# One 512-wide matmul for the high and low token parts of the two convolved up projections, with half of each low weight part made by an adding DMA

## The reference

```python
def conv_ffn(h, w_in, conv_w, conv_b, w_out):
    z = causal_dwconv(h @ w_in, conv_w, conv_b)   # 3 taps per channel, along the tokens
    u, g = jnp.split(z, 2, axis=-1)               # 2816 channels each
    return (jax.nn.gelu(g) * u) @ w_out
```

## Time and profile before

| | |
|---|---|
| median of 3 runs | 1712.98 us |
| the profiled execution | 1715.28 us, of which the span from first to last instruction is 1713.5 us |
| granted TensorE clock, mean | 0.998 |
| PE busy | 1697.4 us (99%) |
| DVE busy | 1380.2 us (81%) |
| ACT busy | 998.8 us (58%) |
| POOL busy | 28.3 us (2%) |
| DMA | 367.06 MB, 214 GB/s over the span |

### The profile page before, as it was taken

How to read it: one execution, slowest core, us unless ns; L and a number is a source line. 1 busy time by engine, 2 the same in 40 slices (tenths; PEclk the granted TensorE clock), 3 DMA queues, 4 the chain that set the end, 5 groups by cost and what they waited for, 6 DMA issues and landing times.

```text
span 1713.5 us, 29104 instructions
## 1 busy us (share of the span) xinstructions
PE 1697.4 (99%) x11410; PEld 1538.4 (90%) x11410; DVE 1380.2 (81%) x2142; ACT 998.8 (58%) x1596; POOL 28.3 (2%) x39
## 2 busy tenths in 40 slices
PE   8999999999999999999999999999999999999999
PEld 8799998999998988889998798888888888698888
DVE  5778888888888888899986879888988876866654
ACT  6565545776554555446678756553655356865542
POOL 0200000000000000000000200000000000000000
PEclk9999999999999999999999999999999999999999
DMA  9345558544547777794552157779687844045552
GB/s 347 136 163 196 180 221 311 190 157 171 196 173 274 277 285 280 281 367 177 173 193 100 50 172 287 277 273 358 241 289 278 312 170 177 27 149 195 195 181 90
DMA packets 62436, 367.06 MB, mean 214 GB/s; under 512 B 6944, under 2 KB 7328, under 8 KB 27776
## 3 DMA queue, kind: packets, MB, share of 16 engines
q1 hardware_dynamic: 61776, 362.70, 58.0%
q0 software_dynamic: 560, 3.01, 0.4%
HBM read 364.64 MB, written 1.05 MB: 213 GB/s over the span
## 4 chain that ended last, share of the span: by engine, by line
PE 92%; DVE 4%; ACT 3%; issue 1%; DMA 0%; SPq 0%; POOLq 0%; DVEq 0%; ACTq 0%; POOL 0%
PE psum L517 18%; PE psum L538 13%; PE psum L390 11%; PE psum L392 11%; PE psum L391 11%; PE psum L519 9%; PE psum L540 6%; PE psum L445 4%; PE psum L507 2%; DVE lo L1934 1%; PE psum L585 1%; ACT hi L1276 1%; PE psum L510 1%; PE psum L986 1%; PE psum L912 1%
## 5 line engine op out<-in xcount | busy, mean ns | idle before, releaser
L1934 DVE TENSOR_TENSOR lo<-raw,hi 128x1024 fp32r<-128x1024 f32 x522 | 621.4, 1229 | 163.0 <-ACT hi L1276 162.9
L1276 ACT ACTIVATE hi<-raw 128x1024 fp32r<-128x1024 f32 x522 | 523.2, 1052 | 334.8 <-PE psum L540 191.5
L517 PE MATMUL psum<-XHL,hi 128*128 128x512 f32 x1280 | 452.5, 399 | 0.0
L390 PE MATMUL psum<-XHL,hi 128*128 128x256 f32 x1320 | 375.9, 285 | 0.1
L391 PE MATMUL psum<-XHL,hi 128*128 128x256 f32 x1320 | 373.5, 283 | 0.0
L392 PE MATMUL psum<-XHL,lo 128*128 128x256 f32 x1320 | 373.5, 283 | 0.0
L519 PE MATMUL psum<-XHL,lo 128*128 128x256 f32 x1280 | 359.5, 281 | 0.0
L538 PE MATMUL psum<-HHL,hi 128*128 (+1 forms) x960 | 338.8, 398 | 0.4 <-DVE S L2124 0.4
L517 PEld LDWEIGHTS psum<-XHL,hi 128*128 128x128 f32 x1280 | 240.5, 188 | 59.9
L540 PE MATMUL psum<-HHL,lo 128*128 (+1 forms) x960 | 269.1, 280 | 0.0
L390 PEld LDWEIGHTS psum<-XHL,hi 128*128 128x128 f32 x1320 | 253.2, 192 | 2.5 <-issue 1.6
(11 more groups left out here) (342 smaller groups left out, 2029.0 us busy)
## 6 DMA issues: line engine op xcount, KB each, us to landing
raw<-slabs_dram SPq DMA_DIRECT2D x269, 1024.0 KB, 5.2
modw<-wmod_dram SPq DMA_DIRECT2D x144, 512.0 KB, 5.4
raw<-slabs_dram SPq DMA_DIRECT2D x4, 512.0 KB, 7.7
A<-small_dram POOLq DMA_DIRECT2D x1, 1536.0 KB, 12.5
X<-x_dram SPq DMA_DIRECT2D x4, 256.0 KB, 4.9
out_dram<-X SPq DMA_DIRECT2D x3, 256.0 KB, 2.3
cond<-cvec_dram POOLq DMA_DIRECT2D x1, 512.0 KB, 7.6
A<-tab_dram POOLq DMA_DIRECT2D x1, 512.0 KB, 15.7
```

The costliest lines, as they stand in the source:

```text
L390: mm(dst, wh, xh, start=start, stop=False, skip_group_check=True)
L517: mm(dst, hi[:, k, j * P:(j + 1) * P], XHL[:, kt, :, :].rearrange("p a t -> p (a t)"), start=start, stop=False, skip_group_check=True)
L1276: f(hi[:, k % SPLIT, at], raw[:, n % RAW, at], ACT.Copy).then_inc(q["hi_ready"], 1)
L1934: v.tensor_tensor(lo[:, k % SPLIT, at], raw[:, n % RAW, at], hi[:, k % SPLIT, at].bitcast(F32), ALU.subtract).then_inc(q["lo_ready"], 1)
```

## The change

The two convolved up stages take the form of the gated ones: `up_stage` goes, and `gated_stage` serves them. ACT copies the low half of each sum (`keep_low`), DVE adds the halves into an SBUF tile (`whole`, tile `WHOLE`, a part of A1), and the taps read this tile instead of PSUM.

For slabs 4 to 21 of each of the two stages (36 slabs, `SHARED`) DVE makes only the first half of `lo`. For the second half ACT writes the negated rounded weights into `lo` (a third pass, `scale=-1.0`), and POOL then issues a DMA that adds `raw` onto them (`accum_op=ALU.add`, 128 x 1024 f32, 512 KB): raw - hi again. PE waits for this DMA before the second half of such a slab, and SP waits for it before it loads into the `raw` buffer. The loops of ACT and DVE in these stages are written out.

```diff
+CONVED = ["f0_up", "f1_up"]
+SHARED = {N0[_name] + _s: 18 * CONVED.index(_name) + _s - 4 for _name in CONVED for _s in range(4, 22)}
...
+        LOWS = [A1[:, 2 * k:2 * k + 2, :].rearrange("p a t -> p (a t)") for k in range(2)]
+        WHOLE = [A1[:, 2 * k + 4:2 * k + 6, :].rearrange("p a t -> p (a t)") for k in range(2)]
...
+        def added(n, i=None):
+            return q[f"lo_added{SHARED[n] % 2}"], plus(16 * (SHARED[n] // 2 + 1), i, 32)
...
+                    if n - RAW in SHARED:
+                        sp.wait_ge(*added(n - RAW))
...
                 for m in range(2):
-                    pe.wait_ge(q["lo_ready"], plus(2 * SPLITS[n] + m + 1, i, 8))
+                    if m and n in SHARED:
+                        pe.wait_ge(q["hi_ready"], plus(2 * SPLITS[n] + 2, i, 8))
+                        pe.wait_ge(*added(n, i))
+                    else:
+                        pe.wait_ge(q["lo_ready"], plus(2 * SPLITS[n] + m + 1, i, 8))
                     for kt in range(KD):
                         last = wide(n, s, m, kt, kt == 0)
                 last.then_inc(q["slab_used"], 1)
...
-                raw_slab(stage, lambda m: psum[:, m, 0:T + 2], T + 2, bank_of_sums)
+                if stage in CONVED:
+                    raw_slab(stage, lambda m: psum[:, m, 0:T], T, bank_of_sums, apart=True)
+                else:
+                    raw_slab(stage, lambda m: psum[:, m, 0:T + 2], T + 2, bank_of_sums)
...
-            def up_stage(stage, preps, bank_of_sums=3):
...
-            up_stage("f0_up", 3, 6)
-            ffn_down("f0_down", "f0_up", [(m, 17) for m in range(4, 8)] + [((N0["f0_up"] + s) % 4, s) for s in range(18, 22)])
+            gated_stage("f0_up", 3, 6)
...
+                if n in SHARED:
+                    f(lo[:, k % SPLIT, HALF:], raw[:, n % RAW, HALF:], ACT.Copy, scale=-1.0).then_inc(q["neg_ready"], 1)
...
-                def pair(p, i=None):
+                def keep_low(s):
+                    act.wait_ge(q["slab_used"], N0[stage] + s + 1)
+                    if s >= 2:
+                        act.wait_ge(*up_count(stage, s - 2))
+                    b = s // 2 % 2 * 4 + s % 2 * 2
+                    f(LOWS[s % 2].rearrange("p (a t) -> p a t", a=2), psum[:, b:b + 2, T:2 * T],
+                      ACT.Copy).then_inc(q["low_kept"], 1)
+                def linear(p, side):
+                    s, b = 2 * p + side, p % 2
+                    if s:
+                        act.wait_ge(*up_count(stage, s))
+                    else:
+                        raw_kept()
+                    if side == 0 and p >= 2:
+                        act.wait_ge(q["h_ready"], HID[DOWN[stage]] + p - 1)
+                    for m in range(2):
+                        k = 2 * p + m + 22 * side
+                        last = f(S[:, b * 1024 + side * 512 + m * T:b * 1024 + side * 512 + (m + 1) * T],
+                                 WHOLE[s % 2][:, m * T:(m + 1) * T], ACT.Identity,
+                                 scale=col(f"fconv{layer}", 88 + k), bias=col(f"fconvb{layer}", k))
+                    last.then_inc(q["lin_ready"], 1)
+                def gelu(p):
                     b = p % 2
-                    for side in range(2):
...
+                    act.wait_ge(q["g_conved"], 11 * layer + p + 1)
                     f(S[:, 2048 + b * 512:2560 + b * 512], S[:, b * 1024 + 512:b * 1024 + 1024],
                       ACT.Gelu_apprx_tanh).then_inc(q["gelu_ready"], 1)
-                pair(0)
...
+                for s in range(22):
+                    if s:
+                        keep_low(s)
+                    split_hi(N0[stage] + s + 2)
+                    linear(s // 2, s % 2)
+                    if s % 2 == 0 and s:
+                        gelu(s // 2 - 1)
+                gelu(10)
...
-                    v.tensor_tensor(lo[:, k % SPLIT, at], raw[:, n % RAW, at],
-                                    hi[:, k % SPLIT, at].bitcast(F32), ALU.subtract).then_inc(q["lo_ready"], 1)
+                    last = v.tensor_tensor(lo[:, k % SPLIT, at], raw[:, n % RAW, at],
+                                           hi[:, k % SPLIT, at].bitcast(F32), ALU.subtract)
+                    last.then_inc(q["lo_ready"], 2 if n in SHARED else 1)
+                    if n in SHARED:
+                        break
...
+                def whole(s):
+                    if s == 0:
+                        dve.wait_ge(q["slab_used"], N0[stage] + 1)
+                        unscaled(WHOLE[0], psum[:, 0:2, 0:T]).then_inc(q["raw_kept"], 1)
+                        return
+                    dve.wait_ge(q["low_kept"], 21 * layer + s)
+                    b = s // 2 % 2 * 4 + s % 2 * 2
+                    v.tensor_tensor(two(WHOLE[s % 2]), psum[:, b:b + 2, 0:T], two(LOWS[s % 2]),
+                                    ALU.add).then_inc(evacuated[s % 2], 1)
+                def taps(p, side):
+                    s = 2 * p + side
+                    dve.wait_ge(q["lin_ready"], LIN[stage] + s + 1)
+                    marks = []
+                    for tap in (1, 2):
+                        for m in range(2):
+                            k = 2 * p + m + 22 * side
+                            at = p % 2 * 1024 + side * 512 + m * T
+                            z = S[:, at + tap:at + T]
+                            if tap == 2:
+                                step.wait(marks[m])
+                            last = stt(out=z, in0=WHOLE[s % 2][:, m * T:(m + 1) * T - tap],
+                                       scalar=col(f"fconv{layer}", (2 - tap) * 44 + k), in1=z,
+                                       op0=ALU.mult, op1=ALU.add)
+                            if tap == 1:
+                                marks.append(step.put(last))
+                    last.then_inc(q["g_conved" if side else "u_conved"], 1)
+                def product(p):
                     b = p % 2
-                    for side in range(2):
...
+                    dve.wait_ge(q["gelu_ready"], 11 * layer + p + 1)
+                    dve.wait_ge(q["u_conved"], 11 * layer + p + 1)
                     buf = S[:, 3072 + b * 512:3584 + b * 512]
-                    hidden(buf, stage, p, i, v.tensor_tensor(
+                    hidden(buf, stage, p, None, v.tensor_tensor(
                         buf, S[:, 2048 + b * 512:2560 + b * 512], S[:, b * 1024:b * 1024 + 512], ALU.mult))
-                pair(0)
...
+                for s in range(22):
+                    whole(s)
+                    split_lo(N0[stage] + s + 2)
+                    if s == 0:
+                        dve.wait_ge(q["raw_kept"], norms[0])
+                    taps(s // 2, s % 2)
+                    if s == 0:
+                        v.memset(tiny[:, 202:203], 0.0).then_inc(evacuated[0], 1)
+                    if s % 2 == 0 and s:
+                        product(s // 2 - 1)
+                product(10)
...
+            def second_halves(stage):
+                at = slice(HALF, SLAB)
+                for s in range(4, 22):
+                    n = N0[stage] + s
+                    k = SPLITS[n]
+                    pool.wait_ge(q["neg_ready"], SHARED[n] + 1)
+                    g.dma_start(lo[:, k % SPLIT, at].bitcast(F32), raw[:, n % RAW, at],
+                                accum_op=ALU.add).then_inc(added(n)[0], 16)
+            for stage in CONVED:
+                second_halves(stage)
```

More of the change, by code:

```diff
@@ L445, in part @@
                         last = mm(dst(m), raw[:, n % RAW, at], source[:, kt, 0:wide],
-                                  start=(kt == 0 and (m == 0 or wide > T)), stop=False, skip_group_check=True)
+                                  start=(kt == 0 and (m == 0 or wide > T or apart)), stop=False, skip_group_check=True)
                     return last
@@ L875, in _ @@
             down_stage("rg_out")
-            up_stage("f1_up", 5)
-            ffn_down("f1_down", "f1_up", [(m, 17) for m in range(4, 8)] + [((N0["f1_up"] + s) % 4, s) for s in range(18, 22)])
+            gated_stage("f1_up", 5)
             gated_stage("g00_up", 6)
@@ L1380, in conv_ffn @@
             def conv_ffn(stage, layer):
-                def pair(p, i=None):
-                    b = p % 2
-                    for side in range(2):
[L1385 to L1393, removed]
-                            act.wait_ge(q["h_ready"], plus(HID[DOWN[stage]] + p - 1, i, 2))
-                        for m in range(2):
-                            k = 2 * p + m + 22 * side
-                            last = f(S[:, b * 1024 + side * 512 + m * T:b * 1024 + side * 512 + (m + 1) * T],
-                                     source[:, m * T:(m + 1) * T], ACT.Identity,
-                                     scale=col(f"fconv{layer}", 88 + k, i, 4),
-                                     bias=col(f"fconvb{layer}", k, i, 4))
-                        last.then_inc(q["lin_ready"], 1)
-                    e, v = up_count(stage, 2 * p + 1)
-                    act.wait_ge(e, plus(v, i, 2))
@@ L2101, in hidden @@
```

(31 more changed lines are left out.)

32 lines of the change are left out of this document (4 added, 28 removed).

## The result

The changed kernel takes 1761.09 us (median of 6 runs, 1760.15 to 1772.43), beside 1712.48 us for the kernel before (6 runs): 1.029 times as long, with a 95% interval of 1.0273 to 1.0307. That is 48.6 us slower. The forecast was 15 us slower with a range up to 1752, so the sign was right and the time lies outside the range.

What follows compares the result with a forecast made beforehand. The prediction took PE, busy 99% of the span, as the bound. A 4.7 us gain against 19.8 us of stalls for the adding DMA gave +15 us: 1728 us on the runs' scale, range 1707 to 1752 us.

Steps and rivals of the forecast that it cites:

- The gain on PE: Convolved up stages: 40 slabs at 5.653 instead of 5.760 us save 4.3 us, plus 0.4 us at the stage ends.
- DVE and ACT fit under PE: Per two slabs of 11.31 us, ACT needs 10.3 and DVE 9.4 us, so both were costed at nothing.
- The margin of 4.7 us: Shared slabs: time from the end of ACT's negated pass until the adding DMA must have landed, or PE stalls.
- The second read: The adding DMA must read both operands, as much as a slab load: 5.0 us alone, 6.5 us beside other loads.
- D = 5.8: Time from the negated pass's end to the add's landing, taken as the middle of 5.0 and 6.5 us.
- 18 x (D - 4.7): PE's stalls in the shared slabs: only every second of 36 pays the add's lateness, 19.8 us in sum.
- The bound of 6.5 from g00_up: Upper end for a two-read add beside other loads, from 6.2 us to landing in g00_up plus 0.3 us for POOL's issue.
- the company of the loads: Adds meet a slab load for about half of their time: a load takes about 4.7 us, adds come every 5.65 us.
- SP's added wait: SP waits for the add before loading; the slab is needed some 9 us after it would land, so costed at nothing.
- rival 1: The add is quick, landing in under 4.7 us, the DMA engines being idle 0.48 of f0_up: 1708 us, chance 0.33.
- PE waits for no load: Behind SP's added wait stands only a load needed some 9 us after it would land, so at no cost.
- Rival 3: The adder or POOL's queue is slower than any load, 7.6 us or more: +47 us, 1760 us, chance 0.10.

Runs made afterwards that it cites:

- e1: Changed kernel without the adding DMA and ACT's third pass, DVE making all of `lo`, the 512-wide form kept: 1708.8 us, 0.9978 of the kernel before.
- e3: Changed kernel with the adds kept, but SP loading only 64 of 2048 columns for 28 slabs whose load comes beside an add: 1721.54 us.
- e5: e1 plus 16 pauses in which PE waits for POOL to clear 768 columns, no adding DMA: 1724.99 us, 1.0054 of the kernel before.
- e8: e1 plus 8 longer pauses in which PE waits for POOL to clear 1792 columns twice, no adding DMA: 1750.07 us, 1.0218 of the kernel before.
- e7: Changed kernel with a plain copy of `raw`, issued by ACT, in place of POOL's adding DMA: 1723.87 us, 1.0049 of the kernel before.

## Why the prediction was wrong in size

- **The gain on PE (4.7 us): right.** e1 shows 3.9 us and the pace of 5.65.
- **DVE and ACT fit under PE: right**, with or without the adds; DVE needed no relief at all.
- **The margin of 4.7 us: right.** An add alone takes 4.5 to 4.6 us plus some 0.3 from the end of the negated pass to the start of the issue, 4.8 to 4.9 in all, and e3 is just late with that, by 0.08 us per slab.
- **The second read: borne out by the engines' time.** An add takes 2.9 us of it, a copy 1.4. The Trainium skill (Collectives: The Full Stack, Part 3, The bandwidth ceiling) says of the ring steps of a collective that an adding step needs two source reads and so runs at half the rate; 2.9 against 1.4 us agrees. The other page weighed there (DMA: Bandwidth & Descriptors, Anatomy of one DMA) gives an estimate of 4.4 us for two reads, and 4.5 for an add alone agrees; the median of 5.5 and the 9.1 beside loads do not.
- **D = 5.8: this is the step that failed, since one middle value stood for all adds.** From the end of the negated pass to the landing, as the prediction defines it, D ran from 4.8 to 9.4 us: 5.9 in the median, but 6.4 in the mean. All 36 adds lie above 4.7, where the formula 18 x (D - 4.7) is linear, so it is the mean that it wants: 18 x 1.66 = 30 us of waits in place of 19.8. The number of waits was close (18 forecast, 19 measured), their size was not: 35.4 / 19 = 1.86 us instead of 1.1. The bound of 6.5 from g00_up was itself a median.
- **Why D was longer:** the company of the loads was put at "about half of its time", where the prediction's own 4.7 us of load in 5.65 is 0.83. Measured are 0.64 and a load beside 35 of the 36 adds. Two things stand behind that. SP's added wait, which I costed at nothing, ties the load to the add: each load goes out as an add lands, which is about when the next add goes out, as at 151.1 us above. And the DMA engines' time was never summed: the idle 0.48 that rival 1 counts on is 2.7 us of a slab, the add takes 2.9. That PE waits for no load is right. e3 shows the price of the company, 39.6 us; whether another tie of the load would help wasn't tried.
- **No term for the clock.** In the two stages of the changed kernel it is 13.7 us, a quarter of what the adds cost. Waits that would be harmless at 0.9 us are not at 3 us (e5 and e8).
- **Rival 3** named 1760 us, with D = 7.6 for every add. The time is right by chance: the mean was 6.4, and the rest came from the clock and the uneven waits. The part of it that holds is that POOL's issue costs something (e7).

The sum with measured terms: -3.9 for the form, +35.4 for the waits, +13.7 for the clock in the stages: +45.2 us. The two profiled spans (1713.5 and 1759.3 us), which both have the late slow stretch, differ by 45.8; the medians differ by 48.6.

## What to carry to other kernels

Cost a new wait by the mean and the spread of what it waits for, not by a middle value: the long ones count most, and here TensorE often paid for them once more in clock. Sum up the DMA engines' time per slab as you sum that of the other engines: 2.9 us of add and 2.9 of load do not fit into 5.65. Before work is moved off an engine, look whether that engine sets the pace at all: here DVE at 96% busy held nobody up, and a transfer that comes out just on time alone will be late beside loads that the same change lets start together with it. The part worth keeping is the 512-wide form alone, 1708.8 us.

## What the runs showed of the hardware

- An adding DMA of 512 KB within SBUF takes 2.9 us of the 16 engines' time, the plain copy 1.4; beside 1,024 KB loads the add lands after 4.5 to 9.1 us, the copy after 2.9 to 7.1.
- POOL's issue takes 0.86 us for an add, at 512 KB as at 256 KB.
- The same plain copy of 512 KB lands after 5.0 us in the median when ACT issues it, 5.6 when POOL does, and the kernel is 18 us faster by the ratios (7.7 us between the profiled spans). The issue takes 0.47 us on ACT and 0.54 on POOL, and starts 0.03 and 0.29 us after the pass that it waits for. The rest can come from when copies and loads meet, which these runs don't tell apart.
- The granted clock in the two stages stayed at 1.00 with 16 waits of 0.85 us, fell after four of eight waits of 1.9 us, and after all of eight of 3.35 us.
